# A two-layer diffusion backbone on one core: down halves tile by tile, tokens first, and gate rows made earlier

## The reference, cut to what matters

```
even:  h  = modulate(rms_norm(x), sh1, sc1) @ w_in        # also for ctx
       x += g1 * (concat(fourier(u), neighbourhood_attention(q, k, v)) @ w_out)
       x += g2 * ((silu(h2 @ w1) * (h2 @ w3)) @ w2)       # dense unit, hidden width 2816
odd:   x += g1 * (concat(gqa_attention, s5_scan) @ w_out) # latent tokens only from here
       x += g2 * moe(h4)                                  # top-2 of 8 experts, hidden width 3584
```

## Time and profile before

| | |
|---|---|
| three runs | 1974.67, 1978.54, 1978.22 us; median 1978.22 |
| profiled execution | 1973.45 us, of which the span of the trace is 1971.7 us |
| TensorE | 1867.4 us busy, 95% of the span; mean granted clock 0.973 |
| VectorE, ScalarE, POOL | 63%, 50%, 15% busy |
| chain that ended last | TensorE 90%, VectorE 4%, issue 2%, ScalarE 2%, DMA 1%, POOL 1% |

### The profile page before, as it was taken

How to read it: one execution, slowest core, us unless ns; L and a number is a source line. 1 busy time by engine, 2 the same in 40 slices (tenths; PEclk the granted TensorE clock), 3 DMA queues, 4 the chain that set the end, 5 groups by cost and what they waited for, 6 DMA issues and landing times.

```text
span 1971.7 us, 25237 instructions
## 1 busy us (share of the span) xinstructions
PE 1867.4 (95%) x8978; PEld 1419.3 (72%) x8978; DVE 1238.1 (63%) x1310; ACT 980.7 (50%) x1068; POOL 301.5 (15%) x592
## 2 busy tenths in 40 slices
PE   5999899899999998878899999999999999999997
PEld 3445554787878785554888888888888888888885
DVE  2121742423333323473698998989989899898996
ACT  2002322431212212244477777767777777777773
POOL 6887701002020212301000000000000000000000
PEclk7999999999999999989799999999999999999998
DMA  9254990222222225231299999999999999999993
GB/s 383 102 216 137 360 366 13 104 75 98 94 86 72 100 86 186 31 130 69 113 356 350 361 369 354 355 348 363 367 356 355 348 361 368 355 355 349 363 367 151
DMA packets 72087, 481.69 MB, mean 244 GB/s; under 512 B 8336, under 2 KB 11536, under 8 KB 17168
## 3 DMA queue, kind: packets, MB, share of 16 engines
q1 hardware_dynamic: 67888, 468.73, 62.3%
q0 software_dynamic: 2448, 7.61, 1.4%
q10 hardware_dynamic: 1680, 4.43, 0.6%
HBM read 473.41 MB, written 7.32 MB: 244 GB/s over the span
## 4 chain that ended last, share of the span: by engine, by line
PE 90%; DVE 4%; issue 2%; ACT 2%; DMA 1%; POOL 1%; ACTq 0%; DVEq 0%
PE bank L955 31%; PE bank L969 15%; PE bank L700 12%; PE bank L729 6%; PE bank L560 6%; PE bank L677 4%; PE bank L767 3%; PE bank L513 2%; PE bank L928 2%; DMA X<-in_ctx 1%; PE bank L938 1%; PE bank L645 1%; PE bank L628 1%; PE bank L992 1%; PE bank L540 1%
## 5 line engine op out<-in xcount | busy, mean ns | idle before, releaser
L1644 DVE TENSOR_TENSOR rest<-ring,WR 128x2048 fp32r<-128x2048 f32 x336 | 758.6, 2288 | 79.3 <-ACT WR L1246 78.3
L1246 ACT ACTIVATE WR<-ring 128x2048 fp32r<-128x2048 f32 x336 | 632.2, 1917 | 50.6 <-DMA ring<-in_experts 50.1
L955 PE MATMUL bank<-WR,xer 128*128 128x512 f32 x1792 | 581.0, 396 | 1.1 <-ACT B L1167 1.1
L955 PEld LDWEIGHTS bank<-WR,xer 128*128 128x128 f32 x1792 | 337.7, 188 | 69.3 <-issue 1.4
L955 PE MATMUL bank<-rest,xer 128*128 128x512 f32 x896 | 350.5, 391 | 0.0
L969 PE MATMUL bank<-WR,heTr 128*128 128x512 f32 x896 | 281.9, 392 | 0.0
L700 PE MATMUL bank<-hTr,WR 128*128 128x512 f32 x704 | 221.9, 397 | 13.2 <-DVE tmpf L1422 12.7
L969 PEld LDWEIGHTS bank<-WR,heTr 128*128 128x128 f32 x896 | 168.2, 188 | 34.3
L955 PEld LDWEIGHTS bank<-rest,xer 128*128 128x128 f32 x896 | 169.3, 189 | 32.7
L969 PE MATMUL bank<-rest,heTr 128*128 128x512 f32 x448 | 174.5, 389 | 0.0
L700 PEld LDWEIGHTS bank<-hTr,WR 128*128 128x128 f32 x704 | 134.3, 192 | 42.9 <-issue 13.9
(11 more groups left out here) (307 smaller groups left out, 1973.5 us busy)
## 6 DMA issues: line engine op xcount, KB each, us to landing
ring<-in_experts SPq DMA_DIRECT2D x336, 1024.0 KB, 4.8
ring<-in_ev_mod SPq DMA_DIRECT2D x24, 1024.0 KB, 9.2
ring<-in_od_mod SPq DMA_DIRECT2D x24, 1024.0 KB, 10.2
ring<-in_ffn_up SPq DMA_DIRECT2D x22, 1024.0 KB, 6.8
ring<-in_ffn_down SPq DMA_DIRECT2D x12, 768.0 KB, 5.3
ring<-in_ev_in SPq DMA_DIRECT2D x8, 1024.0 KB, 11.9
ring<-in_ev_out SPq DMA_DIRECT2D x4, 1024.0 KB, 10.1
ring<-in_od_out SPq DMA_DIRECT2D x4, 1024.0 KB, 13.9
```

The lines of the kernel that those rows point to most:

```text
L955: mm = pe.matmul(bank[m % 2][:, :], xer[:, i, 4 * kh + k, :], w[j][:, 512 * k:512 * k + 512], start=(kh == 0 and k == 0 and x == 0), stop= ...
L1246: act.activation(part(0, h), ring[:, h % HALVES, :], ACT.Copy).then_inc(split_hi, 1)
L1644: dve.tensor_tensor(part(1, h), ring[:, h % HALVES, :], part(0, h).bitcast(F32), ALU.subtract).then_inc(split_lo, 1)
```

## The change

Five edits. (1) SP issues `X` ahead of the weights and holds the first `w_in` slot until `mod` 3 has landed; the scan's tables and `dft` are issued once the first half has landed. The transposes of `xn` go to banks 4 to 7 and stand before `modulation(3)`; ScalarE and VectorE copy them out plain and modulate in place afterwards, and the first product of `w_in_even` waits chunk by chunk. (2) The first dense up unit loops over channel chunks outside and its two banks inside. (3) A down half 1 is one piece: all chunks of a tile, then the next tile, each tile released to VectorE by `down_tile`; the next group's up units wait for two and for all four tiles. (4) After the last unit `normed_tile(2, t)` follows one tile later. (5) Gate rows of `q` = 2 are made in steps 10 and 11, those of `q` = 3 in step 12 and behind the first block of the odd `w_out`, in bank 7.

```diff
@@ -425,7 +426,12 @@
 
+            sp.dma_start(X[:, 0:2, :], a["x"][0].rearrange("(t p) d -> p t d", p=P)).then_inc(x_landed, 16)
+            sp.dma_start(X[:, 2:4, :], a["ctx"][0].rearrange("(t p) d -> p t d", p=P)).then_inc(x_landed, 16)
             for i, (what, n) in enumerate(EARLY):
+                if i == S_IN_E[0]:
+                    for h in (6, 7):
+                        sp.wait_ge(half_landed[h % HALVES], 16 * (h // HALVES + 1))
                 load(i, a["ev_in"][n] if what == "in" else a["ev_mod"][n] if n < 12 else a["od_mod"][n - 12])
@@ -532,12 +538,10 @@
                     k = DC * q + c
-                    if k == 2:
-                        pe.wait_ge(coef_ready, 1)
                     if k >= 4:
...
                     for t in range(tiles):
-                        mm = pe.transpose(bank[k % 4 + (4 if q == 1 else 0)][:, t * P:(t + 1) * P], XN(q, t)[:, c * P:(c + 1) * P], ident)
+                        mm = pe.transpose(bank[k % 4 + (4 if q < 2 else 0)][:, t * P:(t + 1) * P], XN(q, t)[:, c * P:(c + 1) * P], ident)
                     mm.then_inc(xn_turned, 1)
@@ -557,6 +560,8 @@
+                        if j == 0:
+                            pe.wait_ge(h0_act if c % 2 == 0 else h0_dve, c // 2 + 1)
@@ -679,6 +684,8 @@
                         gate_row(gate, b)
+                    if b == 0 and gate == 2:
+                        gate_row(3, 1)
 
@@ -689,13 +696,18 @@
-                        if u and F_ORDER[u - 1][0] == "down":
-                            q = F_ORDER[u - 1][1]
-                            pe.wait_ge(res_gated, r0 + 8 * (q + 1))
-                        for f in range(2):
+                        if n in (6 // 2, 12 // 2, 18 // 2):
+                            pe.wait_ge(res_gated, r0 + 8 * (n // 3) - 2 + 2 * m)
+                        if u == 0:
...
-                                if u == 0 and f == 0:
-                                    pe.wait_ge(ht_lo, c + 1)
+                                pe.wait_ge(ht_lo, c + 1)
+                                for f in range(2):
+                                    for x, (i, j) in enumerate(PASSES):
+                                        mm = pe.matmul(bank[f][:, :], w[i][:, c, f * P:(f + 1) * P],
+                                                       hTr[:, j, c, :], start=(c == 0 and x == 0),
+                                                       stop=(c == DC - 1 and x == 2))
+                        for f in range(2) if u else ():
+                            for c in range(DC):
@@ -704,30 +716,29 @@
+                        if d == 1:
+                            if kh == 1:
+                                continue
+                            pe.wait_ge(split_lo, u + 2)
+                            pe.wait_ge(g_full, k0 + FG[q])
+                            both = [[part(i, 2 * S_FFN + u + x, ks * 512).rearrange("p (k n) -> p k n", k=ks)
+                                     for x in range(2)] for i in range(2)]
+                            for t in range(TILES):
+                                for c in range(FG[q]):
+                                    for x, (i, j) in enumerate(PASSES):
+                                        mm = pe.matmul(bank[t][:, :], gTr[:, i, c, t * P:(t + 1) * P],
+                                                       both[j][c // ks][:, c % ks, :],
+                                                       start=(c == 0 and x == 0), stop=(c == FG[q] - 1 and x == 2))
+                                mm.then_inc(*((down_tile, 1) if t < TILES - 1 else (unit_done, 2)))
+                            continue
...
-                            if d == 0 and q:
-                                pe.wait_ge(res_gated, r0 + 8 * q - 4)
-                            if d == 0 and q == 0:
-                                pe.wait_ge(gate_ready, 8)
-                            if d == 1:
-                                pe.wait_ge(g_full, k0 + FG[q])
-                        if u == F_UNITS - 1:
-                            for t in range(TILES):
-                                for k in range(ks):
-                                    c = ks * kh + k
-                                    for x, (i, j) in enumerate(PASSES):
-                                        mm = pe.matmul(bank[t][:, :], gTr[:, i, c, t * P:(t + 1) * P], w[j][:, k, :],
-                                                       start=False, stop=(c == FG[q] - 1 and x == 2))
-                                if t < TILES - 1:
-                                    mm.then_inc(ffn_tail, 1)
-                        for k in range(ks) if u < F_UNITS - 1 else ():
+                            pe.wait_ge(*((res_gated, r0 + 8 * q - 4) if q else (gate_ready, 8)))
+                        for k in range(ks):
...
-                            if d == 0:
-                                pe.wait_ge(g_lo, k0 + c + 1)
+                            pe.wait_ge(g_lo, k0 + c + 1)
...
-                                    mm = pe.matmul(bank[t + (4 if d == 0 else 0)][:, :],
-                                                   gTr[:, i, c, t * P:(t + 1) * P], w[j][:, k, :],
+                                    mm = pe.matmul(bank[t + 4][:, :], gTr[:, i, c, t * P:(t + 1) * P], w[j][:, k, :],
@@ -739,8 +750,9 @@
                     modulation_turn(s - 1)
+                if s == 2:
+                    norm_turn(0)
             modulation_turn(3)
-            norm_turn(0)
             w_in_even()
@@ -884,8 +896,8 @@
-                if 11 <= r < 13:
-                    gate_row(2, r - 11)
+                if 10 <= r < 13:
+                    gate_row(2 + r // 12, r % 2)
@@ -1009,9 +1022,6 @@
-                if rnd == 0:
-                    gate_row(3, 1)
-                    pe.wait_ge(gate_ready, 12)
@@ -1032,14 +1042,13 @@
             act.dma_start(cst[:, :], a["cst"]).then_inc(cst_landed, 16)
-            act.dma_start(X[:, 0:2, :], a["x"][0].rearrange("(t p) d -> p t d", p=P)).then_inc(x_landed, 16)
-            act.dma_start(X[:, 2:4, :], a["ctx"][0].rearrange("(t p) d -> p t d", p=P)).then_inc(x_landed, 16)
+            act.wait_ge(cond_landed, 16)
+            act.activation(silc, cond.rearrange("p (k s) -> p k s", s=32),
+                           ACT.Silu).then_inc(cond_ready, 1)
+            act.wait_ge(half_landed[0], 16)
             act.dma_start(tail[:, 0:512], a["s5b"]).then_inc(s5_raw, 16)
...
             act.dma_start(dft, a["dft"]).then_inc(dft_landed, 16)
-            act.wait_ge(cond_landed, 16)
-            act.activation(silc, cond.rearrange("p (k s) -> p k s", s=32),
-                           ACT.Silu).then_inc(cond_ready, 1)
 
@@ -1085,7 +1094,17 @@
-            modulate(0)
+            for c in range(0, DC, 2):
+                act.wait_ge(xn_turned, c + 1)
+                act.activation(hT[:, c, :], bank[c % 4 + 4][:, :], ACT.Copy).then_inc(ht_act, 1)
+            act.wait_ge(coef_ready, 1)
+            act.wait_ge(ht_act, 4)
+            for c in range(0, DC, 2):
+                for s in range(2):
+                    o = hT[:, c, s * SEQ:(s + 1) * SEQ]
+                    ins = act.activation(o, o, ACT.Identity, bias=mod[0][:, M_SH1 + c, s:s + 1],
+                                         scale=coef[:, 0, c, s:s + 1])
+                ins.then_inc(h0_act, 1)
@@ -1433,12 +1450,22 @@
-            for s in range(3):
+            modulation_row(0)
+            normed(0)
+            for s in (1, 2):
...
-            normed(0)
+            for c in range(1, DC, 2):
+                dve.wait_ge(xn_turned, c + 1)
+                dve.tensor_copy(hT[:, c, :], bank[c % 4 + 4][:, :]).then_inc(ht_dve, 1)
...
-            modulate(0)
+            dve.wait_ge(ht_dve, 4)
+            for c in range(1, DC, 2):
+                for s in range(2):
+                    o = hT[:, c, s * SEQ:(s + 1) * SEQ]
+                    ins = dve.tensor_scalar(o, o, coef[:, 0, c, s:s + 1], mod[0][:, M_SH1 + c, s:s + 1],
+                                            ALU.mult, ALU.add)
+                ins.then_inc(h0_dve, 1)
@@ -1541,16 +1568,17 @@
-                if what[0] == "down" and what[3] == 1 and u < F_UNITS - 1:
+                if what[0] == "down" and what[3] == 1:
...
-                    dve.wait_ge(unit_done, u + 1)
-                    gated_sum([(d, t) for t in range(4)], 8 + 8 * q + 4 * d, [4, 5, 6, 7] if d == 0 else [0, 1, 2, 3],
-                              tmpf, GF, 8)
-            for t in range(TILES):
-                dve.wait_ge(*((ffn_tail, t + 1) if t < TILES - 1 else (unit_done, F_UNITS)))
-                gated_sum([(1, t)], 4 + RES_FFN + t, [t], tmpf, GF, 8)
-                if t:
-                    normed_tile(2, t - 1)
+                    if d == 0:
+                        dve.wait_ge(unit_done, u + 1)
+                        gated_sum([(0, t) for t in range(4)], 8 + 8 * q, [4, 5, 6, 7], tmpf, GF, 8)
+                    for t in range(TILES) if d else ():
```

(19 more changed lines are left out.)

8 lines of the change are left out of this document (2 added, 6 removed).

## The result

| | before | after |
|---|---|---|
| device time, median of 4 runs | 1977.68 us | 1949.02 us (1946.65 to 1955.1) |
| ratio | | 0.9866, 95% interval 0.9841 to 0.9891 |
| profiled execution: time, span | 1973.45, 1971.7 us | 1946.65, 1944.9 us |
| mean granted clock | 0.973 | 0.981 |

The forecast was 1953.5 (1947 to 1963), a fall of the profiled execution by 24.5 us; it fell by 26.8, and the median by 28.7. I read the trace of after in the order of the prediction. A "stand" is a time in which TensorE stands still.

A forecast was written before the change was run, and what follows sets the result against it. TensorE, busy 95% of the span, bounds the kernel, so gains lie in its stands, late starts and low clock. Terms -19.1 - 2.0 - 0.5 - 1.5 + 0.6 + 0.9 - 2.9 = -24.5 us give 1953.7, taken as 1953.5, range 1947 to 1963.

The forecast's parts named there:

- Down halves, -19.1: Dense unit: gating tile by tile removes 12.7 us of stalls and 6.4 us of low clock after them.
- Both ends of the bound: Down halves in the dense unit: -12.7 us if the clock still dips, -19.1 us if it does not.
- First unit by chunk, -0.5: First dense up unit: its 0.51 us wait for `hTr` goes, since chunk 7 is wanted 9.5 us after the start.
- After the last unit, -2.0: Stand before the third transposes, 7.69 us: the last sum goes ahead of tile 1's norm, saving 2.0 us.
- The front, -1.5: Start of kernel: earlier `xn`, transposes lifting the clock before `mod` 3; first `w_in` product at 44.5 instead of 45.97 us.
- a sign of being wrong: Front: PEclk reading 0.50 at the first `w_in` products would show the forecast wrong.
- The front loses: Rival in the front: transposes do not lift the clock, +4.7 us instead of -1.5, total 1960; chance 0.17.
- The rival's rule: Trainium skill's rule, applied to the front: transposes don't count as matmul activity and full clock does not engage for them.
- Gate rows, -1.4: Moved gate rows: attention's end +0.6, odd `w_out` +0.9, way to the experts -2.9 us.
- VectorE was 5.1 us early: Rival in the dense unit: VectorE gates tiles late past 4.9 us of slip, +9.5 us, total 1963; chance 0.09.
- 18 matmuls into one bank: Rival in halves 1: 18 matmuls in a row into one bank run slower, 1985 at 0.12 us each; chance 0.03.
- The rival at 1950: Rival: clock also rises sooner at the experts and the front is bound by its load alone; chance 0.12.

The follow-up runs named there:

- dense edits alone: The kernel before with only the dense unit's edits, front and gate rows as before; ratio to before 0.9882, span 1951.6 us.
- old down halves: The changed kernel with down halves, first up unit and dense tail as before; ratio to before 0.9982, span 1972.0 us.
- all four tiles: The changed kernel, but the first up unit after each group's down halves waits for four gated sums instead of two; span 1951.5 us.
- the run with transposes in the stands: The changed kernel with PE transposes of a constant filling eight stretches where TensorE stands; span 1942.8 us.
- the best version: The changed kernel without the hold of `w_in` 0, with extra products in eight stands and before `mod` 0 to 2; 1939.98 us, ratio to before 0.9818.

## Why the prediction was right, point by point

The dense edits carry the result, as forecast: -19.1 - 0.5 - 2.0 = -21.6 us, and -23.3 (-19.4 to -27.1) by the medians with the dense edits alone. Front and gate rows together were to give -2.9 and gave -3.6 (-1.6 to -5.5) by the medians with the old down halves. Of these two only the sum is shown; that each came out as forecast in the trace is partly luck, as said below.

- *Down halves, -19.1.* Right in mechanism and size: the unit is 19.95 us shorter, with the 0.5 of its first half in it. Both ends of the bound are separated now: without the stand no low clock (dense edits alone), with a short stand none either (all four tiles), with the long stand it returns (old down halves).
- *First unit by chunk, -0.5.* Its 48 matmuls take 10.93 us without a wait; it was not tested apart.
- *After the last unit, -2.0.* Measured -2.2 (5.47 us in seven traces).
- *The front, -1.5.* The net was right (-1.4), the way was another. I let the clock rise in the transposes; it rose one turn earlier, and fell again at `w_in`, which I had named as a sign of being wrong. That the two cancel (44.5 - 42.9 = 1.6 us sooner, 1.68 us of low clock) is luck. Part of the 1.4 is luck too: against one of the three traces of the old front only 0.4 us is left of it at `mod` 5, and at the dense unit 0.7 us is left on average. The slot `w_in` 0 had 0.4 us to spare, not 3.5. The path that I forecast is that of the run with transposes in the stands: 5.08 us of transposes, `w_in` at 44.92 at full rate, against 4.9 and 44.5.
- *The front loses.* The rival's rule fell: transposes lift the clock and hold it. Its second half (that the clock falls behind the tiny turns) came true, at 1.7 us.
- *Gate rows, -1.4.* The terms came out as +0.5, +0.9, -1.4 and -1.3 us, -1.3 together; that the sum fits is luck. The way to the first expert product was to be 2.9 us shorter and is 1.4. The part behind the gather gained 2.9 us (6.1 instead of 9.0) and the part ahead of it 0.35, but the gather lost 1.8 at half clock (6.56 instead of 4.74 us to the next products). The sum had no term for that. The gather took 5.6 to 6.8 us in six traces with the rows at their new places and 4.8 to 5.6 in three with the old ones. The last -1.3, the clock behind the router, which I had only as a bound, differs as much between traces with the same rows. Without it the rows are worth 0.0 us here.
- *What the sum lacked*, 1.9 us of the 2.3 by which it fell short: the stage from the third transposes to the odd `w_out`. Some 1.5 us of it is the odd attention, and it is not an edit. From the first score product to `w_out` the twelve traces of all kernels here have 71.4 to 73.5 us, with the mean granted clock over the stretch 0.91 in before and 0.95 in after. Why the same stands lower the clock in one execution and not in another is not settled by any run here.

- *Rivals not met:* VectorE was 5.1 us early; 18 matmuls into one bank cost 0.2267 us each, as 3 did. The rival at 1950 lies nearest to the measured 1949.0, but not for its reasons: the front was not bound by its load, and the clock behind the experts' start varies without the edit.

## What to carry to other kernels

Price a stand of TensorE with the low clock behind it, and look at its length: here 4.2 us cost 1.6 to 3.1 us more, 0.9 us cost 0.3. Where several accumulators finish together and one small engine must empty them, finish them one after another, which costs nothing in matmuls. Where a stand can't be removed, products or transposes of a constant kept the clock up here, if they reached close to its end (rests of 0.4 to 1.7 us did no harm here, one of 2.35 us behind fewer products did) and they win time where the stage behind is bound by TensorE. Compare a single term of a sum in several traces before calling it right.

## What was not expected of the hardware

- The clock's answer to a stand differs between executions of the same instructions: `mod` 3's products began at 36.8 to 37.3 us in six traces and at 39.16 in one, with the same TensorE instructions up to there; the low clock behind one stand of 4.2 us was 1.6 us in one kernel and 3.1 us in another. A difference of 2 to 3 us between two single traces shows nothing here.
- Products with few columns seem to let the clock fall although TensorE is busy. In the best version the stands around the 32 products of 1 column after 929.69 are filled, and TensorE stood for 0.42 us only; the first expert products behind them began at full rate (0.40 us), but the clock fell among them (0.89 over 934 to 935, 0.50 over 935 to 938) and one took 0.63 us. That the columns are the cause is argued from this, no run took them out.

```profile
929.69 3.63 PE L1035 MATMUL bank<-s5v,B 128*128 128x1 f32 x32
933.19 0.47 PE L506 MATMUL bank<-cst 128*128 128x128 f32 x2
934.07 0.49 PE L977 MATMUL bank<-WR,xer 128*128 128x512 f32 x1 [0.42 <-issue]
934.40 0.40 PE L977 MATMUL bank<-rest,xer 128*128 128x512 f32 x1
...
935.37 0.63 PE L977 MATMUL bank<-rest,xer 128*128 128x512 f32 x1
```
